# Sample rows of ten projection chunks as two halves of 256 output columns on the two column halves of the array

## The reference

```python
cb, cc, ch, q, k, v, qi, ki, iw = split(rms_norm(h, g) @ w_in)      # 1024 -> 3656
att  = sparse attention over the top keys of an indexer             # qi, ki, iw choose, q, k, v attend
h = h + concat([cb * causal_dwconv3(cc * ch), att]) @ w_out         # 1024 -> 1024
h = h + memory_attention(rms_norm(h, g_mem) @ w_q, mk, mv) @ w_o    # 1024 -> 1024, twice
h = h + (silu(causal_dwconv3(gate) + b) * up) @ w_down              # 1024 -> 2 x 2816 -> 1024
```

## Time and profile before

| | |
|---|---|
| median of 3 runs | 1846.23 us (1844.71 to 1846.78) |
| span of the profiled execution | 1845.1 us |
| PE / PEld busy | 1707.6 / 1187.0 us |
| DVE / ACT / POOL busy | 1114.9 / 811.0 / 733.7 us |
| mean granted TensorE clock | 0.960 |

### The profile page before, as it was taken

The page is one execution under the profiler, slowest core; times in us unless marked ns, Lnnn a source line. Parts: engine busy times, 40 slices in busy tenths (PEclk is TensorE's granted clock), DMA queues, the critical chain, the costliest instruction groups (busy, mean ns, idle before and its releaser), DMA issues.

```text
span 1845.1 us, 33734 instructions
## 1 busy us (share of the span) xinstructions
PE 1707.6 (93%) x13725; PEld 1187.0 (64%) x13803; DVE 1114.9 (60%) x1902; ACT 811.0 (44%) x1476; POOL 733.7 (40%) x704
## 2 busy tenths in 40 slices
PE   6999999996776899989887997999999999999998
PEld 3544445444444655545577544888888888899898
DVE  5856656787797764456655238888788787300000
ACT  5455688655435764432456226435444444110100
POOL 3232365987341200320023426666666666411200
PEclk9999999998797999999988998999999999999999
DMA  7031112023522110301344112121121222321211
GB/s 231 9 109 55 35 45 83 23 81 108 168 90 89 62 38 10 103 1 35 106 154 131 58 52 81 47 70 47 49 68 47 62 54 86 98 95 40 95 38 27
DMA packets 136548, 132.75 MB, mean 72 GB/s; under 512 B 15358, under 2 KB 109630, under 8 KB 136356
## 3 DMA queue, kind: packets, MB, share of 16 engines
q1 hardware_dynamic: 123850, 118.79, 20.7%
q10 hardware_dynamic: 12544, 11.80, 2.0%
HBM read 114.58 MB, written 15.98 MB: 71 GB/s over the span
## 4 chain that ended last, share of the span: by engine, by line
PE 71%; DVE 15%; ACT 6%; issue 4%; POOL 2%; DMA 2%; SPq 0%; ACTq 0%; DVEq 0%; POOLq 0%
PE PS L1558 23%; PE PS L1615 5%; PE PS L1616 5%; PE PS L1617 5%; PE PS L940 4%; PE PS L941 4%; PE PS L942 4%; ACT arena L1631 2%; PE PS L1104 2%; PE PS L1102 2%; PE PS L1103 2%; PE PS L1260 2%; ACT arena L1690 2%; PE PS L1272 1%; POOL arena L2964 1%
## 5 line engine op out<-in xcount | busy, mean ns | idle before, releaser
L1558 PE MATMUL PS<-arena 128*128 128x272 f16 (+1 forms) x3696 | 430.5, 280 | 5.0 <-issue 5.0
L1558 PEld LDWEIGHTS PS<-arena 128*128 128x128 f16 (+1 forms) x3696 | 362.5, 98 | 73.1 <-issue 5.4
L1631 ACT ACTIVATE arena<-PS 128x512 f16<-128x512 f32 (+11 forms) x381 | 189.9, 529 | 235.1 <-PE PS L942 81.3
L1631 ACT ACTIVATE arena<-arena 128x512 f16<-128x512 f32 (+5 forms) x214 | 136.3, 658 | 238.6 <-PE PS L1558 117.1
L368 POOL TENSOR_TENSOR arena<-arena 128x512 bf16<-128x512 f32 (+2 forms) x144 | 161.8, 1158 | 184.1 <-ACT arena L359 183.8
L940 PE MATMUL PS<-arena 128*128 128x512 f16 (+3 forms) x648 | 228.1, 362 | 5.2 <-DVE arena L2597 1.4
L941 PE MATMUL PS<-arena 128*128 128x512 f16 (+3 forms) x648 | 227.5, 361 | 0.0
L1615 PE MATMUL PS<-arena 128*128 128x256 f16 (+1 forms) x792 | 216.0, 273 | 1.4 <-POOL arena L918 1.0
L1617 PE MATMUL PS<-arena 128*128 128x256 bf16 (+1 forms) x792 | 215.9, 273 | 0.0
L1616 PE MATMUL PS<-arena 128*128 128x256 f16 (+1 forms) x792 | 215.9, 273 | 0.0
L942 PE MATMUL PS<-arena 128*128 128x512 bf16 (+2 forms) x608 | 212.0, 359 | 0.0
(11 more groups left out here) (351 smaller groups left out, 3693.6 us busy)
## 6 DMA issues: line engine op xcount, KB each, us to landing
arena<-w_gu SPq DMA_DIRECT2D x44, 512.0 KB, 4.8
arena<-w_down SPq DMA_DIRECT2D x8, 1408.0 KB, 7.8
arena<-w_in SPq DMA_DIRECT2D x8, 1024.0 KB, 5.1
arena<-w_kv_mem SPq DMA_DIRECT2D x8, 1024.0 KB, 7.2
arena<-cache_mem_k SPq DMA_DIRECT2D x32, 256.0 KB, 3.4
arena<-cache_mem_v ACTq DMA_DIRECT2D x28, 256.0 KB, 3.9
arena<-w_in SPq DMA_DIRECT2D x24, 256.0 KB, 3.8
arena<-x_prompt SPq DMA_DIRECT2D x9, 512.0 KB, 6.3
```

Source lines behind the costliest of these rows:

```text
L1558: mm = e.matmul(PS[:, product_bank(f, i) + c, 0:TC], w[:, i, k], s[i][:, q, c, :], start=first, stop=last)
L1631: e.activation(out, in_, ACT.Copy, **kw).then_inc(sem(name), 1)
```

## The change

For the sample tile, the 512 output columns are cut in two: columns 0 to 255 go to partitions 0 to 63 of the PSUM bank, columns 256 to 511 to partitions 64 to 127, both at columns 0 to 255 of the bank. Each matmul becomes two with the same stationary operand and half the moving one, which stand on columns 0 to 63 and 64 to 127 of the array. All that reads such a bank does it in two instructions; the second raises the semaphore. Nothing else changes: no wait, no order, no transfer.

```diff
+        def sides(bank):
+            return [(PS[g * NS:(g + 1) * NS, bank, 0:256], slice(g * 256, (g + 1) * 256)) for g in range(2)]
+
+        def tile_parts(j, bank):
+            return sides(bank) if j == NB else [(PS[:, bank, :], slice(0, 512))]
+
+        def lin_samples(e, bank, x_hi, x_lo, wh, wl, ks, last=KT - 1):
+            for q, k in enumerate(ks):
+                for x, w in ((x_hi, wh), (x_lo, wh), (x_hi, wl)):
+                    for out, cs in sides(bank):
+                        mm = e.matmul(out, x(k)[:, SEQ:T], w[:, q, cs], start=(k == 0 and x is x_hi and w is wh),
+                                      stop=(k == last and w is wl))
+            return mm
+
+        def lin_tile(e, j, bank, x_hi, x_lo, wh, wl):
+            if j == NB:
+                return lin_samples(e, bank, x_hi, x_lo, wh, wl, range(KT))
+            return lin(e, PS[:, bank, :], x_hi, x_lo, wh, wl, range(KT), tcols(j))
...
+                if j == NB:                                        # value_step
+                    mm = lin_samples(e, 4 + j % 4, lambda k: xa_hi[:, k, :], lambda k: xa_lo[:, k, :],
+                                     A.high(A_V)[:, k:k + 1, :], A.low(A_V)[:, k:k + 1, :], [k])
...
+                if j == NB:                                        # output_part
+                    mm = lin_samples(e, 2 + L % 2, lambda k: out_x(k)[0], lambda k: out_x(k)[1], wh[:, k0:k0 + 2, :],
+                                     wl[:, k0:k0 + 2, :], (k0, k0 + 1))
...
-                e.activation(squares[0:n, L % 2, :], PS[0:n, out_bank(L), :], ACT.Square).then_inc(sem("s2_raw"), 1)
+                for out, cs in tile_parts(ITEMS[L][1], out_bank(L)):
+                    x = e.activation(squares[0:n, L % 2, cs], out, ACT.Square)
+                x.then_inc(sem("s2_raw"), 1)
...
-                copy(v_f32[0:n, j % 2, :], PS[0:n, 4 + j % 4, :], "v_f32")
-                copy(v_hi[0:n, j, :], PS[0:n, 4 + j % 4, :], "v_ev")
+                for to, name in ((v_f32[0:n, j % 2, :], "v_f32"), (v_hi[0:n, j, :], "v_ev")):
+                    for out, cs in tile_parts(j, 4 + j % 4):
+                        x = e.activation(to[:, cs], out, ACT.Copy)
+                    x.then_inc(sem(name), 1)
...
-                e.tensor_tensor(v, PS[0:rows(j), L % 4, :], v, ALU.add).then_inc(sem("l8_ev"), 1)
+                for out, cs in tile_parts(j, L % 4):
+                    x = e.tensor_tensor(v[:, cs], out, v[:, cs], ALU.add)
+                x.then_inc(sem("l8_ev"), 1)
```

More of the change, by code:

```diff
@@ L994, in project_item @@
                     A.ready(e, c)
-                mm = lin(e, PS[0:rows(j), out_bank(L), 0:w], lambda k: xa_hi[:, k, :], lambda k: xa_lo[:, k, :],
-                         A.high(c), A.low(c), range(KT), tcols(j))
+                if c == A_KI:
+                    mm = lin(e, PS[0:rows(j), out_bank(L), 0:w], lambda k: xa_hi[:, k, :], lambda k: xa_lo[:, k, :],
+                             A.high(c), A.low(c), range(KT), tcols(j))
+                else:
+                    mm = lin_tile(e, j, out_bank(L), lambda k: xa_hi[:, k, :], lambda k: xa_lo[:, k, :],
+                                  A.high(c), A.low(c))
                 mm.then_inc(sem("s2_mm"), 1)
@@ L1709, in _ @@
                         e.wait_ge(sem("s2_roped"), L - 2)
-                    copy(raws[0][0:n, L % 3, 0:w], PS[0:n, L % 2, 0:w], "s2_raw")
+                    if c == A_QI and j == NB:
+                        (out, cs), (out2, cs2) = sides(L % 2)
+                        e.activation(raws[0][0:n, L % 3, cs], out, ACT.Copy)
+                        copy(raws[0][0:n, L % 3, cs2], out2, "s2_raw")
+                    else:
+                        copy(raws[0][0:n, L % 3, 0:w], PS[0:n, L % 2, 0:w], "s2_raw")
                     if L == 0:
@@ L1940, in _ @@
                         e.wait_ge(sem("q7_tp"), upto("q7_tp", L - 2))
-                    copy(qraw[0:n, L % 3, :], PS[0:n, L % 4, :], "q7_raw")
+                    for out, cs in tile_parts(L6[L][1], L % 4):
+                        x = e.activation(qraw[0:n, L % 3, cs], out, ACT.Copy)
+                    x.then_inc(sem("q7_raw"), 1)
                 if L >= 2:
@@ L2215, in item_gain @@
                     e.wait_ge(sem("s2_roped"), L - 2)
[L2216 to L2219, removed]
+                for out, cs in tile_parts(j, out_bank(L)):
+                    x = e.tensor_tensor(raws[1][0:n, L % 3, cs].rearrange("p (a d) -> p a d", d=HD),
+                                        out.rearrange("p (a d) -> p a d", d=HD),
+                                        qkg[0:n, int(c == A_K), :][:, None, :].broadcast_to(
+                                            [n, (cs.stop - cs.start) // HD, HD]), ALU.mult)
+                x.then_inc(sem("s2_gn"), 1)
             def item_norm(L):
@@ L2551, in early_output @@
                 e.wait_ge(sem("xp_ld"), upto("xp_ld", 16 * (NEARLY - 1 if j > 1 else NEARLY)))
-                e.tensor_tensor(v, PS[0:rows(j), 2 + L % 2, :], v, ALU.add).then_inc(sem("l6_ev"), 1)
+                for out, cs in tile_parts(j, 2 + L % 2):
+                    x = e.tensor_tensor(v[:, cs], out, v[:, cs], ALU.add)
+                x.then_inc(sem("l6_ev"), 1)
             for m in range(NA + 4):
```

21 lines of the change are left out of this document (13 added, 8 removed).

## The result

The changed kernel takes 1836.74 us (median of five, 1830.67 to 1838.72) against 1846.23 of the kernel before: ratio 0.9944, 95% interval 0.9928 to 0.9959. Two more sets of runs of the same file gave 0.9935 (0.9918 to 0.9952) and 0.9938 (0.992 to 0.9956). It is faster, by some 10 us where 17.25 were forecast. The median lies inside the stated range of 1825.5 to 1842, and outside the 1826 to 1833 that the prediction called the likeliest. The profiled span fell from 1845.1 to 1835.4.

A forecast was written before the change was run, and what follows sets the result against it. TensorE was taken to bound the kernel (71% of the path), with all gains due before 1148 us. Item terms summed to 17.25 us off the 1845.1 span, plus 1.1 for the median: 1829.0 us, range 1825.5 to 1842.

The forecast's parts named there:

- one load exposed: Rival on the matmul pairs: one weight load not hidden, pair 0.137 us, kernel about 1832.3 us; chance 0.10.
- no overlap: Rival on the matmul pairs: halves do not run at once, pair 0.218 us, kernel 1847.3 us; chance 0.10.
- in turn: Rival on the matmul pairs: loads and streams all one after another, pair 0.274 us, kernel about 1859 us; chance 0.08.
- 1: Indexer queries, ending at 83.9 us: TensorE delivers earlier until VectorE itself is late; gain 1.6 us.
- 2: Values, 157.2 to 168.0 us: eight steps between dot products each shorten by 0.32; gain 2.4 us.
- 3, 4: Attention queries and keys: TensorE then waits for POOL and VectorE, gain 0; split instructions cost 0.2 us together.
- 5: Output, first half, within the attention loop, 667.3 to 676.5 us, TensorE always busy; gain 2.5 us.
- 6: Output, second half, ending at 792.6 us: gain 1.95 us, limited by ScalarE's root before the norm.
- 7: Memory queries, first half: ScalarE waits for these products, nothing else near the bound; gain 2.5 us.
- 8: Memory queries, second half, last item of its stage: VectorE waits 1.57 us for it; gain 1.5 us.
- 9 and 10: Memory output, two sample items in a row, 1070.6 to 1081.0 us: all shift together; gain 5.0 us.
- the clock: TensorE's granted clock: one half-clock fall more or less worth up to 1.7 us; 3 us either side, no chance given.

The follow-up runs named there:

- e4: Changed kernel with all 24 matmuls of the first half ahead of all 24 of the second; 1845.18 us, ratio 0.9998 to the kernel before.
- e8: Changed kernel plus the down projection's four sample tiles as pairs of 128 columns; 1817.43 us, ratio 0.9858 to the kernel before.
- e11: Changed kernel with the down projection's sample tiles also in halves, but values, queries and keys whole; 1818.51 us, ratio 0.9856 to the kernel before.
- e5: Changed kernel with the sample items of attention queries and keys made whole again; 1833.04 us, ratio 0.9914 to the kernel before.
- e6: Kernel before with only output projection, memory queries and memory output (items 5 to 10) as halves; 1833.52 us, ratio 0.9922 to the kernel before.
- e9: The changed kernel run again unchanged, for a third profile; 1834.8 us, ratio 0.9938 to the kernel before.
- e2: Changed kernel plus nine filler matmuls with unused results ahead of the sample scores; 1831.8 us, ratio 0.9916 to the kernel before.
- e3: Kernel before plus nine filler matmuls with unused results ahead of the sample scores; 1850.2 us, ratio 1.0016 to the kernel before.
- e7: Changed kernel with the values' sample item made whole again; 1830.91 us, ratio 0.9916 to the kernel before.
- e12: Changed kernel with each item's matmuls ordered by threes per half instead of alternating one by one; 1837.11 us, ratio 0.9944 to the kernel before.
- e1: The changed kernel run again unchanged, for a second profile; 1835.36 us, ratio 0.9935 to the kernel before.

## Why the prediction was right, and where its sum was not

**The pair's pitch: right.** 0.109 forecast and measured. All three rivals on the overlap are out: one load exposed would have shown 0.137, no overlap 0.218 (e4 shows what that looks like: 4.75 us an item and a time equal to before), in turn 0.274. The nearest row, two row halves, was the right guide. The rule of the Trainium skill, page "TensorE: Matmul & The Clock Gate", section "Part 3: Packing small matmuls", that a load overlaps only matmuls of another row group, isn't followed here: both halves use all rows, and both loads hide behind 0.109 and, in e8, behind 0.056.

**Item by item**, from the ledger, forecast and then measured:
- 1: 1.6; measured 2.0 at 86 us, and 0.2 to 0.6 of it left at 157. The step itself was right: VectorE now takes the rotation without a wait, where the earlier trace rows had one of 1.62. Then the granted clock took some back: 0.69 over 11 us in both the changed kernel and e11, below, against 0.84 before.

```profile
81.92 0.67 DVE L2292 TENSOR_TENSOR arena<-arena,turns 64x512 f32<-64x512 f32 x1
```

```profile
83.00:94.00 11.00, 8.58 (x49) 5.50 (x49) 4.30 (x16) 0.61 (x2) 0.00 (x0) 0.69 0.52 136
```

```profile
84.00:95.00 11.00, 8.93 (x97) 5.95 (x98) 5.68 (x19) 2.78 (x7) 0.00 (x0) 0.84 0.29 74
```

(The first fence is the changed kernel's VectorE timeline, the second a window of e11, the third of the kernel before.)
- 2: 2.4; 2.5 at 168, less 0.33 for the wait before the scores that grew from 0.27 to 0.71: 2.2. The reason given was right too: VectorE now runs three dot products back to back, where the earlier trace rows shows a wait of 0.45 before one:

```profile
158.36 4.12 DVE L2368 SCALAR_TENSOR_TENSOR arena<-arena,iwt 128x1024 f32<-128x1024 f32 x3 [1.31 <-ACT arena L1782]
162.94 2.70 DVE L2368 SCALAR_TENSOR_TENSOR arena<-arena,iwt 128x1024 f32<-128x1024 f32 x2 [0.46 <-ACT arena L1782]
```

- 3, 4: -0.2; -0.7 to -0.9. The waits grew as said, to 3.47 for POOL (3.5 forecast) and 5.19 for VectorE (6.6 forecast), in place of those of the earlier trace rows:

```profile
369.58 2.81 PE L958 MATMUL PS<-arena 128*64 128x256 f16 x48
376.45 0.59 PE L940 MATMUL PS<-arena 128*128 128x512 f16 x1 [3.47 <-POOL arena L368]
```

```profile
434.24 0.61 PE L1149 MATMUL PS<-arena 128*128 128x512 f16 x1 [5.19 <-DVE arena L463]
```

  What the zero left out is that a longer wait can bring the clock down, and the first matmuls behind it then run slower. With the two items whole the gain moves by less than 0.1 between 339 and 427.9 us (e5, e6, e11).
- 5: 2.5; 2.5 in every profile of the table.
- 6: 1.95; 2.5 at once, of which 0 to 1.2 goes again by 845 (not taken apart). VectorE's wait of 2.96 is 0.40 now:

```profile
791.40 0.86 DVE L2665 TENSOR_TENSOR arena<-PS,arena 64x256 f32<-64x256 f32 x2 [0.40 <-PE PS L958]
```

- 7: 2.5; 2.56. 8: 1.5; 2.56 less 0.89, so 1.67. 9 and 10: 5.0; 5.0 in every profile, from 1065 to 1087.

Taken from e8's profile, which met no fall at 170 us, the ten come to 17.6 us. With its own 13.9 from the down projection taken off, that execution would have been 1813.11 + 13.9 = 1827.0 us, and 1829.6 without the 2.6 us that it was ahead before the first changed item, against the 1829.0 forecast.

**The term that failed: the clock.** "One more or one less is worth up to 1.7 us where TensorE is the bound. I put 3 us to either side for it. It is a width, not a case." It was a case. The prediction had the pieces, a fall and the remark that everything later moves against the chip's own steps, but it took one fall of 3.4 us as the size. One fall lasted 17.1 or 20.5 us, and the stretch it hit is TensorE's alone, so 7.7 to 9.4 us were lost (e9, e5), about half of what all ten items bring. That falls can be this long stood in the profile of the kernel before, which has TensorE at half clock through this window:

```profile
552.00:572.00 20.00, 12.66 (x117) 8.07 (x118) 10.89 (x22) 8.00 (x19) 2.27 (x2) 0.50 0.60 204
```

The starts that the prediction named show the same: the long piece came 10.6 us earlier and not 17, and the convolution projections 3.0 later and not 4.0 earlier. The time is in the range all the same because its upper part was kept for loads or overlaps that go half wrong, and these did not; the sum's fault of some 8 us fell into room left for another. That much of being right was luck. And the look for danger went to items 3 and 4, where waits of several us were foreseen, and not to waits of 0.7 us ahead of the f32 scores. That the clock and no other thing took the 8 us is shown by three roads: the rows at 0.50 to 0.54 with the starts 1.07 apart for 0.59; e2 against e3; and e8, e7, e6 and e11, which keep their gain through 185 whenever the clock stays up.

The prediction's test, that the shift at 345 be still there at 560, looked past the place: at 345 the shift was already -5.6. From 345 to 560 it goes from -5.6 to -2.4 in the changed kernel, from 4.6 to 5.6 in e8, 0.2 to 0.1 in e6 and 2.1 to 0.2 in e11, so that stretch moves the gain by up to 3 us either way, and doesn't take it back.

**Open.** What makes the fall come: it needs neither longer waits (e8 and the changed kernel have the same 0.71 and 0.68) nor another program. The five profiles with a fall reached the first score at 168.78 to 169.62, e8 at 167.55, but e4 at 169.57 without one, so the place in the program's time doesn't decide by itself. Counted from where the half-clock stretch near 86 us began, the five come to that score after 82.8 to 83.3 us, e8 after 82.0, e4 after 80.1. In each of the five the fall begins 85.3 us after the start of that stretch. That fits the prediction's remark, but no run held all else fixed and moved that alone. How often it comes is open too; single times without a profile can't be assigned.

## What to carry to other kernels

Where a matmul's rows fill only half of the array's columns, split its output columns over the two halves and interleave the two streams one by one or in groups of three: the time of such items halves, down to 128 moving columns. Leave alone those items behind which the engine waits for another anyway. And price the clock as a case, not as a width: after every shift, list the stretches where TensorE alone is the bound and comes out of even a short wait, and take half their length as the stake.

## What the runs showed of the hardware that was not expected

- Matmuls on the free column half start ahead of others before them in the program, of three at e4's seam and of two in e12's groups of three, without a loss.
- Two loads of 64 weight columns hide behind 0.056 us of streaming (e8), with pairs 0.003 us apart.
- The same program met or escaped a half-clock stretch of 17 to 20 us at one place (after, e1, e9 against e8), and was shifted by 0.4 to 2.6 us already before the first changed instruction, by 78 us.
- Going from 128 to 64 weight columns and back costs some 0.1 us each way here. In the values' bursts of the changed kernel, the timeline below, the first half starts 0.31 after the dot product's last matmul, where the pitch is 0.22, and the next dot product 0.45 behind it, where three pitches of a pair are 0.33.

```profile
161.40 0.38 PE L1091 MATMUL PS<-arena 128*128 128x512 f16 x1
161.71 0.52 PE L958 MATMUL PS<-arena 128*64 128x256 f16 x6
162.16 0.39 PE L1090 MATMUL PS<-arena 128*128 128x512 f16 x1
```
